# A chain of one transformer block and two hybrid layers: two memory projections moved to the kernel's start, and x transposed on TensorE

## The reference

```python
h = _modulate(_rms_norm(x, norm1_g[l]), shift1, scale1)          # first norm
lru_x = h @ w_in[l][:, :2048]                                    # "lrux" in the kernel
...
x = x + gate1 * (merged @ w_out[l])
h2 = _modulate(_rms_norm(x, norm2_g[l]), shift2, scale2)         # norm 0 of the kernel
x = x + gate2 * (square(relu(h2 @ w_ff1)) @ w_ff2)
x = _rms_norm(x, final_g)                                        # norm 1
for l in range(2):                                               # hybrid layers
    kv = mem @ w_mem_kv[l]                                       # mem does not depend on x
    k_mem, v_mem = split(kv, 2, axis=-1)
    ...
    x = layer_norm(ALPHA * x + y, ln_gain, ln_bias)              # norm 2, norm 3
```

## Time and profile before

| | us |
|---|---|
| median of 3 runs (lowest, highest) | 2683.52 (2682.26, 2683.72) |
| the profiled execution | 2681.57 |
| its span, first to last instruction | 2679.7 |
| TensorE busy | 2634.5 (98%) |
| VectorE, ScalarE busy | 1840.7 (69%), 1372.3 (51%) |
| granted TensorE clock, mean | 0.996 |

### The profile page before, as it was taken

The page is one execution under the profiler, slowest core; times in us unless marked ns, Lnnn a source line. Parts: engine busy times, 40 slices in busy tenths (PEclk is TensorE's granted clock), DMA queues, the critical chain, the costliest instruction groups (busy, mean ns, idle before and its releaser), DMA issues. The chain is left out here.

```text
span 2679.7 us, 35468 instructions
## 1 busy us (share of the span) xinstructions
PE 2634.5 (98%) x13754; PEld 2228.5 (83%) x13754; DVE 1840.7 (69%) x2517; ACT 1372.3 (51%) x2027; POOL 75.8 (3%) x129
## 2 busy tenths in 40 slices
PE   7999999999999999999999999999999999999997
PEld 6788787778888888888888888888888888888886
DVE  7776988886888765665566665766566656765665
ACT  2157666554445655445544555544555545445543
POOL 0000000000000000000000000100000001000000
PEclk9999999999999999999999999999999999999998
DMA  9974777878888685565555554655446556654463
GB/s 390 409 258 150 257 254 248 283 271 323 303 308 321 228 266 201 189 199 191 185 193 198 189 177 167 204 185 181 158 156 205 189 179 194 212 177 169 142 222 123
DMA packets 163622, 593.22 MB, mean 221 GB/s; under 512 B 19296, under 2 KB 20576, under 8 KB 162816
## 3 DMA queue, kind: packets, MB, share of 16 engines
q1 hardware_dynamic: 157536, 570.86, 62.1%
q0 software_dynamic: 5344, 18.74, 2.2%
q10 hardware_dynamic: 576, 1.37, 0.1%
HBM read 583.49 MB, written 2.16 MB: 219 GB/s over the span
## 5 line engine op out<-in xcount | busy, mean ns | idle before, releaser
L1527 DVE TENSOR_TENSOR both_w<-raw,both_w 128x1024 fp32r<-128x1024 f32 x848 | 1023.0, 1217 | 545.0 <-ACT both_w L1112 541.0
L1112 ACT ACTIVATE both_w<-raw 128x1024 fp32r<-128x1024 f32 x848 | 881.5, 1049 | 611.4 <-PE bank L799 343.6
L836 PE MATMUL bank<-H,both_w 128*128 128x512 f32 x3232 | 777.1, 391 | 0.2 <-DVE XC L2007 0.2
L836 PEld LDWEIGHTS bank<-H,both_w 128*128 128x128 f32 x3232 | 592.8, 188 | 117.8 <-issue 2.9
L848 PE MATMUL bank<-H,both_w 128*128 128x256 f32 x3232 | 440.4, 285 | 3.2 <-DVE both_w L1527 3.2
L848 PEld LDWEIGHTS bank<-H,both_w 128*128 128x128 f32 x3232 | 420.1, 191 | 24.6 <-DVE both_w L1527 4.1
L794 PE MATMUL bank<-both_w,H 128*128 128x512 f32 x1024 | 257.1, 393 | 0.0
L794 PE MATMUL bank<-both_w,F 128*128 128x512 f32 x1024 | 252.9, 389 | 0.0
L1579 DVE SCALAR_TENSOR_TENSOR raw<-raw,CR 128x1024 f32<-128x1024 f32 x192 | 232.7, 1218 | 22.1 <-DMA raw<-in_ada 20.7
L794 PEld LDWEIGHTS bank<-both_w,H 128*128 128x128 f32 x1024 | 190.0, 188 | 43.4 <-issue 3.8
L794 PEld LDWEIGHTS bank<-both_w,F 128*128 128x128 f32 x1024 | 192.2, 188 | 39.9
(11 more groups left out here) (309 smaller groups left out, 2413.2 us busy)
## 6 DMA issues: line engine op xcount, KB each, us to landing
raw<-in_w_in SPq DMA_DIRECT2D x296, 512.0 KB, 3.3
raw<-in_w_ff SPq DMA_DIRECT2D x256, 512.0 KB, 4.3
raw<-in_ada SPq DMA_DIRECT2D x192, 512.0 KB, 5.4
raw<-in_w_out SPq DMA_DIRECT2D x96, 512.0 KB, 4.5
raw<-in_w_sig SPq DMA_DIRECT2D x64, 512.0 KB, 5.1
raw<-in_w_vw SPq DMA_DIRECT2D x48, 512.0 KB, 4.1
raw<-in_w_x SPq DMA_DIRECT2D x32, 512.0 KB, 15.5
raw<-in_w_lru_out SPq DMA_DIRECT2D x32, 512.0 KB, 4.9
```

Of the source, the lines that this page charges most:

```text
L836: ins = pe.matmul(out[i].rearrange("p (a s) -> p a s", a=2), whi[:, s, at_:at_ + 128], both[:, :, kt, :], start=(c == 0 and k == 0), stop= ...
L1112: act.activation(whi[:, s, 0:el.n], raw[el.slot][:, 0:el.n], ACT.Copy).then_inc(s_hi, 1)
L1527: dve.tensor_tensor(wlo[:, s, 0:n], raw[el.slot][:, 0:n], v32(whi[:, s, 0:n]), ALU.subtract).then_inc(s_lo, 1)
```

## The change

- Two units `pre` 0 and 1 (8 whole chunks each) compute the memory values of both layers before everything else. They read memory as `MS`, loaded as four more pieces and split into `Hhi`/`Hlo`, the space that x's halves take later. Their results go to a buffer `STAGE` and by GpSimd's transfers to DRAM (`values`); before each layer GpSimd reads that layer's back into `VM`. The units `vm` are gone.
- The first norm works from x by tokens (`RT`, four quarters of 512 KB, loaded within the stream). ScalarE squares with a running sum, VectorE forms factors for 2 columns, and two matmuls of ones by diagonal matrices (`DG`) spread them over partitions (`Rv`). TensorE transposes x, 8 transposes for each of 4 groups, and VectorE multiplies out of PSUM into `XR`. `RES`, the ones-matmul sums and the later load of `RT` are gone.
- The stream: memory, values' weights, c, x and the modulation pieces of blocks 0 and 1 first, interleaved; then four pieces for block 2; from block 3 on as before, a weight and two modulation pieces in turn. Six lrux weights, not four, come after the last block. The first block's halves are swapped.
- The filling of the norms: norm 0 has `km` 0, norm 1 has `km` 1, norm 2 has `km` 2 and 3.
- The norms lose one tick in ScalarE's, VectorE's and TensorE's order; the third and fourth transposed groups wait for the `spread_out` of the groups that had their banks, not for the rounding; norm 1 takes the form of the others.
- The remaining 128 modulation pieces: none for 8 chunks at norm 0 where there were 16, then 0.72 a chunk where it was 0.65.

The diff, cut to its core:

```diff
+    for l in range(2):
+        unit("pre", l, "vw", l, "MS", **whole)
-    for b, half in [(b, half) for b in range(NB - 2) for half in range(2)] + [(14, 0), (15, 0), (14, 1), (15, 1)]:
-        if half == 0:
+    for b, half in [(0, 1), (0, 0)] + [(b, half) for b in range(1, NB - 2) for half in range(2)] + [(14, 0), (15, 0), (14, 1), (15, 1)]:
+        if b and half == 0:
             mark("norm1", b)
...
     unit("km", 0, "kv", 0, "M0")
-    unit("km", 1, "kv", 1, "M0")
...
     mark("norm", 1)
-    unit("vm", 0, "vw", 0, "M0", **whole)
+    unit("km", 1, "kv", 1, "M0")
...
-            unit("vm", 1, "vw", 1, "M1", **whole)
...
+    first = [(c0 + b, half) for b in range(2) for c0 in (16, 0) for half in range(2)]
+    for n in range(16):
+        if n < 8 and n % 2 == 0:
+            stream.append(Elem("mem", CH, ("mem", 2, n // 2), g=2, kt=n // 2))
+        weight(early[n // 8], n % 8)
+        if n < 2:
+            inputs[len(stream)] = [("c", n)]
+        elif n == 3:
+            inputs[len(stream)] = [("x", i) for i in range(4)]
+        if 4 <= n < 12:
+            modulation(*first[n - 4])
+            if n % 4 == 3:
+                first_end.append(len(stream) - 1)
+    for b in range(2, NB):
...
         for c0 in (16, 0):
-            if b > 1:
+            if b > 2:
                 weight(parts.pop(0), 0)
...
-                due += 0 if n < 72 or 264 <= n < 280 else 0.5 if n < 136 else 0.65
+                due += 0 if n < 88 or 280 <= n < 288 else 0.5 if n < 152 else 0.72
...
+        def first_norm():                                  # TensorE
+            yield from ticks(8)
+            pe.wait_ge(s_cst, 16)
+            pe.wait_ge(s_dg, 2)
+            for t in range(2):
+                ins = pe.matmul(pT[:, t * 128:t * 128 + 128], ones, DG[:, t, :], start=(t == 0), stop=(t == 1), skip_group_check=True)
+            ins.then_inc(s_rb, 1)
+            held["T"] = (s_rvb, 1)
+            for g in range(4):
...                                                        # clear the group's banks, wait for x
+                for b in range(4):
+                    for t in range(2):
+                        ins = pe.transpose(out[:, b, t * 128:t * 128 + 128], RT[:, t, 512 * g + 128 * b:512 * g + 128 * b + 128],
+                                           ident)
+                ins.then_inc(s_xg, 1)
...
+                yield
...
+        def first_norm():                                  # VectorE
+            yield from ticks(6)
+            t = statistics(-1)
+            root_step(-1)
+            dve.wait_ge(s_rv, 1)
+            dve.wait_ge(s_cst, 16)
+            for t in range(2):
+                dve.tensor_scalar(DG[:, t, :], ident, RN[:, t:t + 1], None, ALU.mult).then_inc(s_dg, 1)
+            yield from ticks(3)
+            dve.wait_ge(s_rb, 1)
+            dve.tensor_copy(Rv, pT[:, 0:256]).then_inc(s_rvb, 1)
+            dve.wait_ge(s_rvb, 1)
+            for g in range(4):
+                dve.wait_ge(s_xg, g + 1)
+                dve.tensor_tensor(XR[:, 4 * g:4 * g + 4, :], turned_group(g), over(Rv, 4), ALU.mult).then_inc(s_xr, 1)
+                yield
...
         def turned(n):
             src = RT if n else SCL
-            yield
             for g in range(4):
                 yield
                 out = turned_group(g)
-                if g % 2:
-                    clear("T")
-                    clear("O")
-                else:
-                    clear("S")
+                if g < 2:
+                    for name in "TO" if g else "S":
+                        clear(name)
+                else:
+                    pe.wait_ge(s_ea, 4 * n + g - 1)
+                    pe.wait_ge(s_ed, 4 * n + g - 1)
...
+            if un.kind == "pre":                           # GpSimd
+                pool.wait_ge(s_ev["pre"], un.j + 1)
+                pool.dma_start(values_d[un.j], STAGE[:, :, :]).then_inc(s_vst, 16)
...
+                    if st[2] in (1, 2):                    # GpSimd, at the marks of norms 1 and 2
+                        l = st[2] - 1
+                        pool.wait_ge(s_vst, 32)
+                        pool.wait_ge(s_pv, 32 + 16 * l)
+                        pool.wait_ge(*last_use[5])
+                        pool.dma_start(VM[:, :, :], values_d[l]).then_inc(s_vmr, 16)
```

More of the change, by code:

```diff
@@ L237, in _plan @@
     due = 0
+    early = [s[1] for s in steps if s[0] == "unit" and s[1].kind == "pre"]
     parts = [s[1] for s in steps if s[0] == "unit" and s[1].part]
-    for b in range(NB):
+    first = [(c0 + b, half) for b in range(2) for c0 in (16, 0) for half in range(2)]
+    inputs = {}
+    for n in range(16):
[11 more added lines that the diff above has]
+    for b in range(2, NB):
         if b == 13:
@@ L256, in _plan @@
             stream.append(Elem(s[0], CH, s, g=s[1], kt=s[2]))
-        elif s[0] == "unit" and not s[1].part:
+        elif s[0] == "unit" and not s[1].part and s[1].kind != "pre":
             for c in range(s[1].nkc):
@@ L297, in _plan @@
             un.bank = 4 * un.j
+            if un.part == "open" and un.j == 0:
+                un.after = ("pre", 2)
         else:
@@ L313, in _plan @@
             holder[un.bank // 2] = (un.kind, un.n + 1)
-    return steps, units, stream, done, order, first_end
+    return steps, units, stream, done, order, first_end, inputs
 def _jobs():
@@ L524, in _build @@
     gdram = nc.dram_tensor("gtab", (32, 384), F32, kind="Internal").ap()
+    values_d = nc.dram_tensor("values", (2, 128, 2, 512), F32, kind="Internal").ap()
     gates_d = nc.dram_tensor("gates", (2, NB, 128), F32, kind="Internal").ap()
@@ L610, in _build @@
                 mem_no[el.g, el.kt] = n_split
-    first_split = sum(el.kind == "w32" for el in stream)
+    lru_end = 1 + max(el.ord for el in stream if el.kind == "w32")
+    earlier, in_slot = {}, {}
+    for el in stream:
+        if el.kind == "w":
+            earlier[el.ord] = in_slot.get(el.ord % NSP, -1)
+            in_slot[el.ord % NSP] = el.ord
     last_use = {el.slot: (s_freed[done[i][0]], done[i][1]) for i, el in enumerate(stream)}
@@ L1036, in small @@
             held["T"] = (s_cq, l + 1)
-        pe.wait_ge(s_cst, 16)
-        for j in range(8):
-            pe.wait_ge(s_sq, j + 1)
-            src = TG[:, j % 2, :]
-            pe.matmul(pS[:, 0:256], ones, src[:, 0:256], start=(j == 0), stop=False, skip_group_check=True)
-            pe.matmul(pS[:, 0:256], ones, src[:, 256:512], start=False, stop=(j == 7),
-                      skip_group_check=True).then_inc(s_st, 1)
-        held["S"] = (s_inv, 1)
+        side.start(first_norm())
         for st in steps:
@@ L1308, in spread_out @@
             act.wait_ge(s_tz, 4 * n + g + 1)
-            if n == 1:
-                for i in range(4):
-                    b = 4 * g + i
-                    act.activation(Hhi[:, b, :], out[:, i, :], ACT.Copy, scale=v(V_FG + b)).then_inc(s_hh, 1)
-                return
             if g >= 2:
@@ L1322, in spread_out @@
                                          bias=mod[:, 48 + b:49 + b])
+                elif n == 1:
+                    ins = act.activation(work(g)[:, i, :], out[:, i, :], ACT.Copy, scale=v(V_FG + b))
                 else:
@@ L1365, in evac @@
             ps, j, kind = banks[un.bank], un.j, un.kind
+            if kind == "pre" and j == 1:
+                norm1(0)
             if kind not in ("res", "y"):
@@ L2098, in vector @@
         decay_begin()
-        feed(first_end[0] - 1)
-        root()
-        feed(first_end[0])
-        newton()
-        dve.wait_ge(s_rv, 1)
-        scaled(0)
+        side.start(first_norm())
         for st in steps:
```

179 lines of the change are left out of this document (86 added, 93 removed).

## The result

The kernel after takes 2689.79 us, the median of 13 runs (2688.00 to 2691.95), against 2682.94 for the kernel before on the same chip (13 runs, 2682.04 to 2683.76): ratio 1.0025, 95% interval 1.0017 to 1.0032, so 6.9 us slower. The forecast was 2687, with 3.3 us lost. The time is inside the range; the loss is twice the forecast, and it lies a little past the 0.2% up to which I had called it no change.

The account below looks back on a forecast made before the run. TensorE, busy 2634.5 of 2679.7 us, bounds the kernel; transfers bound the start. -10.3 + 6.2 + 8.0 - 0.6 = +3.3 on the profiled 2681.57 gives 2684.9, plus 2 for the median: 2687, range 2677 to 2694.

Parts of the forecast that it names:

- Start: From the beginning to the first q chunk: bound by transfers, q at 180.6 us, 10.3 us won.
- cover of 1.7: At the start, the us by which TensorE's work may end later, as transfers set the end.
- rival 2: Start brings less: early chunks hang on VectorE, pre units end at 75, lrux at 185.5; +8, 2692; chance 0.12.
- The 1.3 us for each write of the staged values: At the start, each of two 512 KB writes of staged values takes a piece's time of transfer, 1.3 us.
- Norm 0: First inner norm, filling cut from 8 chunks to 4: TensorE waits 4.5, 1.3, 1.5, 0.6; 6.2 us lost.
- Group 0's low half: At norm 0, VectorE's subtraction ready at 880.4, filling starting at 861.90; TensorE waits 4.5 us for it.
- Norm 1: Second inner norm, filling cut from 8 whole chunks to 4: 33.9 against 25.9 us, 8.0 lost.
- Norm 2: Third inner norm, filling cut from 16 chunks to 8: nothing new waits, 0.6 us won.
- Free edits: Values' reread, modulation pieces at 0.72 a chunk (0.09 us more VectorE in 2.72), swapped first halves: no cost.
- Rival 1: Clock falls to half in the norms' new pauses: +2.3 at both, up to 2.3 at first norm; 2691; chance 0.20.
- Rival 3: Inner norms hidden by faster ScalarE and VectorE, first group by 877, each losing 3 or less: 2677; chance 0.18.
- Rival 4: First chunks wait for c or x, pre units only replace lrux time, taking all the 10.3: 2697; chance 0.03.

Follow-up runs that it names:

- e4: The kernel after, with VectorE copying the first norm's factors and scaling its first group one tick earlier; the median doesn't move.
- e5: The kernel after, with nine unread matmuls before the first reader of H3 and of H4, filling TensorE's pauses; median 0.8 us lower, not told from nothing.
- e6: The kernel after, with modulation pieces at 0.60 then 0.65 a chunk instead of 0.50 then 0.72, same 8-chunk window; no time won.
- e8: The kernel after, with modulation pieces at 0.50 then 0.86 a chunk, none in the last two res units; median 1.8 us lower, interval reaching over 1.
- e1: The kernel after, with modulation pieces at the old 0.65 a chunk and none for 16 chunks at norm 0; 7.5 us slower.
- e3: The kernel before with the norm part alone: four filling chunks at norms 0 and 1, new norm form, old start; 25.9 us lost.
- e7: e3 with modulation pieces at 0.60 then 0.65 a chunk and an 8-chunk window without them; 2700.71 us, 17.0 over the kernel before.
- e2: The kernel before with modulation pieces at 0.72 a chunk for 0.65 and nothing else; median 3.2 us up, ratio 1.0011.
- c1: The kernel before with only layer 1's values first, the new first norm, eight filling chunks per inner norm, old piece rate; 1.4 us under the kernel before.

## Why the prediction held, and where it didn't

- *Start, -10.3*: -9.7. The waits of 2.8 and 3.8 are 3.20 and 3.36, chunk 8 ends at 39.0 (39.2 said), q at 181.4 (180.6 said). Not in the working: the first matmul comes at 8.69, not 7.4, and eight matmuls at half speed behind the second wait, 1.4 us; with these the pre units end at 70.6, not 68.4. As the transfers would have held q at about 180 anyway (e4, e5, e6, e8), only 0.8 of it reaches q and 0.6 the term, which is the cover of 1.7 that rival 2 was told of. The 1.3 us for each write of the staged values was right. The DMA view of the kernel after over 74 to 80 us, with the second write (POOL's queue is q0; packets, MB, share of 16 engines):

```profile
q1 hardware_dynamic: 542, 1.96, 80.9%
q0 software_dynamic: 144, 0.52, 21.4%
```

The write takes 21.4% of 6 us, 1.28 us, the first one 14.3% of the 9 us from 43 to 52, 1.29. The total stays at 415 and 414 GB/s, as before it (407 from 66 to 74), so the weights' queue gives way. The Trainium skill ("Trainium Kernel Development and Optimization", Key Constraints) has the queues of SP, ScalarE and GpSimd on the same 16 DMA engines, and this trace agrees.
- *Norm 0, +6.2*: +7.0. Group 0's low half was forecast 18.5 us behind the filling's start; it is 18.6. The later groups' waits are 0.94 and 0.41, not 1.3, 1.5 and 0.6; the slow matmuls take the place of the difference and 0.7 more; in the runs whose clock stayed low for less (e1, e6, e8) the term would be 6.3.
- *Norm 1, +8.0*: +7.7 (8.5 to 8.6 in e3, e4 and e7, where the clock stayed low for longer). *Norm 2, -0.6*: -0.4, with the one wait of 1.2 forecast (1.18 at 2166.32).
- *Free edits*: this step failed, in the sentence on the ada pieces at 0.72. I priced them on VectorE alone, 0.09 us of 2.72, with 9 of 60 us to spare. The stretch lost 5.3 us in the profiled execution, 3.0 in e4 and 5.7 in e5, which have the same pieces, and 3.2 in e2 without the rest. The resource was another: in the last res units the transfers were already at 0.93 of their time before the change, mem pieces and ada pieces beside the weights, and there ScalarE leaves its splits for 6 us to begin a norm. The stock of split weights must last that long, and it did so with little to spare (some 0.2 us in e1). The new schedule puts a modulation piece directly ahead of the last weight that is split before the statistics; every profile with that order has a wait of 1.5 to 2.3 there, and in the kernel after the clock fell behind it, 1.7 more. That this one place is what tips it fits all profiles but was not tried by itself. I had read one window, 687 to 747, and took its cover for the whole stretch. In the sum, 3.3 + 5.3 + 1.7 for the rest is the 10.3 of the profiles; in the medians the error is about 3.6.
- *Rival 1*, the clock: it falls, in norm 0 to 0.50 as in the earlier trace rows, behind a pause of 4.28 us. The mechanism was right, its price wrong: 0.7 and 0.1 in place of 2.3 each (e5), because what follows waits for ScalarE and VectorE anyway. Where no wait follows it has its full price: the 1.7 us behind the wait at 885.61, a place that the rival didn't name. The Trainium skill ("TensorE: Matmul & The Clock Gate", What's actually happening) has half clock as the idle engine's default, and the rows agree.
- *Rival 2*, less at the start: lrux 2.2 late, 0.8 of it seen. *Rival 3*, hidden norms: no, the first group comes at 18.6. *Rival 4*: no.

The 2687 stands nearer to 2689.8 than the mechanism deserves: 2 us were added to the sum of 2684.9 because three runs had a median that much over the profiled one, and with thirteen runs that distance is 1.4. That the medians differ by 6.9 and not by the 10.3 of the profiles helped too. So the number was in part luck.

## What to carry to other kernels

Filling in front of a chain on other engines is worth as much as the chain is long, here 18.5 us from the norm's start: moving it elsewhere pays only for the surplus. When units move, whatever is paced by counting them moves too: look up who reads the last of it (here the gate rows), and price the faster pacing at the fullest place it passes, on the transfers and on every engine's written order, not in an average window. Look there not only at how many transfers there are but at which one stands directly ahead of the one that is waited for. And a slow clock behind a pause costs only what the next wait doesn't swallow: up to 1.0 us in front of a chain on other engines, 1.7 in the middle of TensorE's own work.

## What the runs showed of the hardware

The clock fell behind pauses of TensorE of 4.28 us (0.50), 4.06 (0.61 over 1647.3 to 1650.4), 3.36 (0.57 over 50.9 to 54.5) and even 2.18 us in the res unit (0.72 over 886 to 892). The length of the pause doesn't settle it alone. In the kernel after the pause of 3.20 at 42.24 left the next eight matmuls at 2.09. In e5, whose order is the same up to there, one of 3.19 at 42.28 was followed by eight in 3.76, at a clock of 0.50 over 44.8 to 48.4. And the wait of 1.80 to 1.82 us for VectorE's split shortly before the first attention scores (286.93 in the kernel before, 320.74 in the kernel after) stands in all twelve profiles: behind it the clock was half in e3, e6 and c1 (0.50 over 320.0 to 323.4 in e6) and full in the other nine.

The first eight matmuls of the kernel took 3.78 us, twice their time, though the window's clock reads 1.00:

```profile
8.70:12.40 3.70, 3.70 (x9) 2.93 (x10) 2.29 (x2) 1.96 (x2) 0.00 (x0) 1.00 1.03 410
```

That 1.00 is no reading. The records of the granted clock in this trace begin at 13.03 us, and where there is no record the view shows full clock. The durations are those of half clock: eight such matmuls took 3.75 at 919.51 and 3.76 in e5, at 0.50.
